# TensorE takes four steps of a weight stream ahead of a state space loop

## The reference, cut to what matters

```python
z = rms_norm(x, norm1_w) @ w_in            # 256 x 2048 @ 2048 x 8192
y_ssm = s5_mixer(z[:, :1024], ...)         # a linear recurrence over 256 tokens, 64 groups of 64 complex states
y_attn = diff_attention(q, k, v, ...)      # 8 heads, two softmaxes each, p0 - lam * p1
m = sigmoid(gs) * (y_ssm @ w_proj_ssm) + sigmoid(ga) * (y_attn @ w_proj_attn)
x = x + m @ w_out                          # then a gated feed-forward layer, then the second block
```

## Time and profile before

| | us |
|---|---|
| median of 3 runs | 2527.08 (2525.64 to 2527.29) |
| the profiled execution, its own time | 2526.77 |
| its span in the profile | 2525.0 |
| PE busy | 2460.2 (97%) |
| DVE busy | 1475.3 (58%) |
| ACT busy | 1129.0 (45%) |
| POOL busy | 186.0 (7%) |
| DMA, mean over the span | 163 GB/s |

### The profile page before, as it was taken

How to read it: one execution, slowest core, us unless ns; L and a number is a source line. 1 busy time by engine, 2 the same in 40 slices (tenths; PEclk the granted TensorE clock), 3 DMA queues, 4 the chain that set the end, 5 groups by cost and what they waited for, 6 DMA issues and landing times.

```text
span 2525.0 us, 45210 instructions
## 1 busy us (share of the span) xinstructions
PE 2460.2 (97%) x19625; PEld 2249.2 (89%) x19625; DVE 1475.3 (58%) x1814; ACT 1129.0 (45%) x1562; POOL 186.0 (7%) x198
## 2 busy tenths in 40 slices
PE   7999999999999999999999999999999999999997
PEld 7777888999889999999988899899888898999885
DVE  4899955565444545445444445745645567456555
ACT  5565555544444444444443344423544535234542
POOL 4000000001000000000000001310100051201000
PEclk9999999999999999999999999999999999999998
DMA  8444444454545555565555576423537664235465
GB/s 235 133 150 147 149 142 132 128 182 166 200 149 182 179 184 181 186 184 184 185 191 191 192 221 176 118 86 116 163 107 239 173 216 135 86 102 151 127 199 167
DMA packets 259414, 412.43 MB, mean 163 GB/s; under 512 B 53072, under 2 KB 74064, under 8 KB 258704
## 3 DMA queue, kind: packets, MB, share of 16 engines
q1 hardware_dynamic: 254496, 395.57, 50.7%
q0 software_dynamic: 4400, 13.89, 2.0%
q10 hardware_dynamic: 320, 0.08, 0.0%
HBM read 403.17 MB, written 6.30 MB: 162 GB/s over the span
## 4 chain that ended last, share of the span: by engine, by line
PE 90%; DVE 6%; ACT 2%; issue 1%; POOL 0%; DMA 0%; ACTq 0%; SPq 0%; DVEq 0%
PE bank L561 88%; DVE wp_lo L1069 2%; ACT wp_hi L1722 1%; PE bank L768 0%; DMA xt<-x 0%; DVE r_a L1548 0%; DVE rsd L1194 0%; DVE nsd L1461 0%; DVE r_kb L1550 0%; ACT L1722 0%; PE bank L662 0%; DVE xr L1715 0%; DVE xr L1713 0%; DVE sqr L1204 0%; POOL sgsA L2170 0%
## 5 line engine op out<-in xcount | busy, mean ns | idle before, releaser
L1069 DVE TENSOR_TENSOR wp_lo<-raw,wp_hi 128x1024 fp32r<-128x1024 f32 x740 | 921.0, 1251 | 893.9 <-ACT wp_hi L1722 893.5
L1722 ACT ACTIVATE wp_hi<-raw 128x1024 fp32r<-128x1024 f32 x740 | 782.5, 1060 | 1123.5 <-PE bank L561 1096.0
L561 PE MATMUL bank<-XX_hi,wp_hi 128*128 128x256 f32 x3840 | 1113.0, 290 | 10.8 <-DVE wp_lo L1069 9.7
L561 PE MATMUL bank<-XX_lo,wp_hi 128*128 128x256 f32 x3840 | 1087.5, 283 | 0.0
L561 PE MATMUL bank<-XX_hi,wp_lo 128*128 128x256 f32 x3840 | 1087.2, 283 | 0.0
L561 PEld LDWEIGHTS bank<-XX_hi,wp_hi 128*128 128x128 f32 x3840 | 736.6, 192 | 29.5 <-DVE wp_lo L1069 12.6
L561 PEld LDWEIGHTS bank<-XX_lo,wp_hi 128*128 128x128 f32 x3840 | 737.1, 192 | 2.2 <-issue 1.9
L561 PEld LDWEIGHTS bank<-XX_hi,wp_lo 128*128 128x128 f32 x3840 | 736.5, 192 | 0.0
L561 PE MATMUL bank<-wp_hi,FF_hi 128*128 128x512 f32 x352 | 137.3, 390 | 0.0
L561 PE MATMUL bank<-wp_hi,FF_lo 128*128 128x512 f32 x352 | 137.1, 389 | 0.0
L561 PE MATMUL bank<-wp_lo,FF_hi 128*128 128x512 f32 x352 | 137.1, 389 | 0.0
(11 more groups left out here) (476 smaller groups left out, 2774.7 us busy)
## 6 DMA issues: line engine op xcount, KB each, us to landing
raw<-w_in SPq DMA_DIRECT2D x304, 512.0 KB, 3.8
raw<-w_out SPq DMA_DIRECT2D x96, 512.0 KB, 4.1
raw<-w_ffn_gate SPq DMA_DIRECT2D x88, 512.0 KB, 3.8
raw<-w_ffn_up SPq DMA_DIRECT2D x88, 512.0 KB, 4.3
raw<-w_ffn_down SPq DMA_DIRECT2D x88, 512.0 KB, 3.6
raw<-w_proj_attn SPq DMA_DIRECT2D x16, 512.0 KB, 4.0
raw<-w_proj_ssm SPq DMA_DIRECT2D x16, 512.0 KB, 3.6
raw<-w_glu SPq DMA_DIRECT2D x8, 512.0 KB, 3.4
```

The costliest lines, as they stand in the source:

```text
L561: return e.matmul(o, lhsT, rhs, start=start, stop=stop, skip_group_check=True)
L1069: return tt(d, src, hi, SUB)
L1722: return e.activation(o, x, func, bias=bias, scale=scale)
```

## The change

TensorE's program takes three more steps ahead of `s_weights(0)` and one behind it, two instead of four after the loop, and two more ahead of the attention turns. No other engine's program is changed, and neither is any buffer or wait.

```diff
             last.then_inc(CPJ.made("c", t), 1)
 
+        main(at.go(3))
         s_weights(0)
+        main(at.go(1))
         for t in range(16):
             i, r = t // 2, 2 * (t % 2)
             if t == 0:
@@ -735,7 +737,7 @@
             if r == 0 and i < 7:
                 s_weights(i + 1)
             main(at.share(4.3))
-        main(at.go(4))
+        main(at.go(2))
         at.limit("ga3")
         s_result(15)
 
```

## The result

The changed kernel takes 2657.95 us (median of 4 runs, 2655.74 to 2658.85) against 2527.18 for the kernel before (4 runs, 2525.64 to 2528.19): a ratio of 1.0517, 95% interval 1.0503 to 1.0531. It is 130.8 us slower. The profiled execution took 2658.32 with a span of 2656.5.

The account below looks back on a forecast made before the run. TensorE, busy for 97% of the span, was taken to bound the kernel. Start and loop 75.1, behind it - 1.7 + 6.9 + 4.3, clock + 33.8 = 118.4 us; with 2526.8 that gave 2645 us, range 2585 to 2690.

Parts of the forecast that it names:

- The rule that decides: In the loop, VectorE's splits cover six steps; TensorE four ahead has one or two in hand, closing a loop of waits.
- Ahead of the loop: Before turn 1: early steps fill the 3.74 us gap, then a 6.0 us stall; 1.1 us of the gaps filled is left.
- In the loop: Turns 1 to 15: one stall in odd turns, two in even; loses 76.2 us, less 1.1 from the start: +75.1.
- Behind the loop: Attention part: gap ahead of scores filled, -1.7 us; stalls in four score turns, +6.9; wait before step 260, +4.3.
- The clock: TensorE drops to 1.2 GHz behind 13 idles of 3.7 us or more, 2.6 us each: +33.8 us; shorter idles cost 0.
- Every idle lowers the clock: Rival: all 24 idles lower TensorE's clock, 62.4 us in place of 33.8: 2674 us, or 2688 at 3.2 each; chance 0.18.
- The clock stays up: Rival: TensorE's clock doesn't fall behind the idles, leaving 84.6 us: 2611 us; chance 0.12.
- The wait for `CPJ` doesn't bind: Rival: in the loop, even turns cost as odd ones, 18.2 us: about 2580 to 2585 us; chance 0.06.
- The lead is free: Rival: low parts are ready early in every half-turn, so filled gaps save 9.7 us: 2517 us; chance 0.07.

Follow-up runs that it names:

- Run 6: Kernel before, with TensorE, VectorE and ScalarE all taking four steps ahead early, none extra ahead of the scores: 2532.46 us, ratio 1.0023.
- Run 7: Changed kernel plus matmuls whose product nothing reads, placed where TensorE would idle in the loop: 2632.69 us, ratio 1.0417 against the kernel before.
- run 8: Kernel before, TensorE taking three steps ahead of the loop and two ahead of the scores, entered as not due and given back: 2523.26 us, 0.9983.
- run 9: Kernel before, TensorE taking only three steps early ahead of the loop and giving them back, none ahead of the attention: 2530.20 us, ratio 1.0008.
- a lead of two: Kernel before, with TensorE taking two steps ahead of the state space loop and keeping that lead through it: 2547.60 us, ratio 1.0081.

## Why the prediction was right

It was right in sign and mechanism, and 13 us short of 2658, within its range. By its steps:

- **The rule that decides.** It held. Run 6 is the proof: the same early steps without a distance between the engines bring no waits in the loop, and the first step of distance is free while the next ones are not.
- **Ahead of the loop.** Steps 33 to 36 filled the gap; then a stall of 5.35 us, predicted 6.0; `BPJ` of turn 1 began at 101.25 and ended some 102.3, predicted 100.5. The low clock behind the stall can make that difference: it reaches to 89.6, which from 85.89 on loses 1.9 us. It reaches turn 1 by way of ScalarE, whose copies of the weights wait for TensorE's transposes and stand ahead of its next high parts; VectorE's split at 94.30 waits 2.59 us for them, and TensorE 1.73 us for the split. The prediction had put ScalarE's high parts at nothing, and here they counted.
- **In the loop.** Counted were 75.1 us for start and loop. The pattern came as described, one stall in odd turns and two in even ones, 2.75 and 4.48 in turn 2 (2.8 and 4.45), 76.6 us of waits for splits and 3.2 for `vM` between 88 and 446 us ("some 80 us"). Run 7 shows the term that was mis-sized: handshakes set to nothing were 8.4 us. (The turns as listed add up to 306.8 and not 306.5 us, which changes nothing.)
- **Behind the loop.** The gap ahead of the scores was given as -1.7 and gave -1.9. The four score turns with a stall of 1.7 are there, 1.8 to 1.9 us each, at 491.55, 522.92, 564.74 and 594.02, 7.2 us in place of 6.9. The wait ahead of step 260 was predicted as one of 4.9 us and came as 1.03 and 2.08, with 1.03 in an earlier turn. With the 0.59 of before taken off, 3.5 for 4.3. Together with the clock I gave this part 13.8, and it took 19.4: 11.5 of idles more than before, 5 of clock (next point), and some 3 that I have not traced.
- **The clock.** "The rows show nothing between 1.73 and 3.74 us ... I take 0" is the step that failed. The four stalls of 1.8 to 2.1 us at 491.55, 522.92, 594.02 and 638.06 were followed by 3.4 us at 1.2 GHz; that at 564.74, 1.76 us long, was not. These two windows of the change are the first of them, at its mean of 0.72:

```profile
486.00:491.00 5.00, 3.79 (x28) 1.00 0.26 85
491.00:497.00 6.00, 5.45 (x33) 0.72 0.60 162
```

  In the loop the other half of the step failed the other way: 16 drops in place of 12, but each cost less than the 2.6 us taken. With the start they cost 28.6 (26.8 and 1.8), 1.8 each, and 31.2 was predicted. That the sum is near is luck: more drops and cheaper ones cancel. The 16 stretches last 71.7 us, half of which would be 35.9. A part of a slow stretch lies beside a wait that is there anyway, as in turn 2, where the window up to 138.10 has 0.94; "the loss counts in full" denied that.
- **The rivals.** "Every idle lowers the clock" at 2.6 each gave 2674, and the time lies between it and the forecast: 16 drops at some 24 idles. The Trainium skill, page "TensorE: Matmul & The Clock Gate", section "HAM oscillation - how this bites in real kernels", describes a loop whose wait, 3 to 5 us long there, lowers the clock anew in each round. This case agrees in kind and in most rounds, not in all. The prediction applied it to all 24 idles, though the eleven of 2.8 to 3.05 us lie at or below the shortest of the page's waits. "The clock stays up" is what run 7 makes of the loop: it has 2632.7, and this rival said 2611. Of the 21.7 us between, 8.4 are the handshakes and some 7 the attention's four drops, which run 7 leaves in; the rest isn't traced. "The wait for `CPJ` doesn't bind" is refuted by 37.1 us of waiting at its line. "The lead is free" holds for one step of lead.

In figures: 118.4 predicted, 131.5 in the spans. Start and loop 75.1 + 8.4 of handshakes, clock in them 31.2 predicted and 28.6 measured, behind the scores' gap 13.8 predicted (6.9, 4.3, a drop of 2.6) and 19.4 measured, the gap -1.7 and -1.9, the rest 0 and 1.9, of which 1.7 is the drop behind 638.06.

## What to carry to other kernels

Where engines run one list of work in order and one prepares a fixed number of pieces ahead of another, the distance between their places is a budget. Before moving work forward on one engine, count the smallest slack there (0.7 us at step 72 here) and look whether the preparing engine waits in the same round for signals that the move delays: then the loss comes back in every round, not once. To fill a single gap, lend the steps and give them back in the share that follows (4 us won in run 8, none in run 9), or move the places of all engines together, and then look for the stage behind that isn't ready early (run 6 lost its gain there).

## What I had not expected of the hardware

Idles of only 1.7 to 2.8 us can be followed by 1.2 GHz: 3.4 us each behind 1.76 and 1.85 us in the attention turns of the changed kernel, and 10.2 us behind 1.7 us in run 9. With a lead of two, waits of 1.76 us (127.74) and 1.85 us (265.04) in a loop that is otherwise full were followed by 6.8 and 3.4 us. The same wait of 1.7 us in the kernel before (granted clock 1.00 from 358 to 375 us), and that of 1.76 us at 564.74 in the changed one, were not. And adding matmuls that nothing reads (538 of them between 95 and 400 us, busy for 67.7) made the changed kernel 25 us faster, by keeping the clock at 2.4 GHz.
